# One unit's square, two masks and a turn moved in the delta-rule part of a decoder layer on one core

## The chip, the core and the metric

The kernel runs on one core of a Trainium2 chip. The metric is the device time of one execution in microseconds (us); the time before is the median of 3 runs. The engines are TensorE (PE: matmuls and turns, that is transposes), VectorE (DVE), ScalarE (ACT), GpSimd (POOL) and SyncE (SP, which issues loads). Each takes its instructions in the order of its own list and waits at semaphores for the others.

## The reference, cut to what matters

One inference step of a hybrid decoder layer for 256 prompt tokens and 8 samples of 8 tokens: RMSNorm, one input projection, then two groups of heads side by side (8 attention heads, and 8 heads of a gated delta rule behind a causal convolution of width 4), an output projection, and a convolutional feed-forward part. The change lies in the delta-rule heads:

```
q, k, v = silu(causal_conv4(qkv, conv_w, old_rows))      # and the new old_rows are an output
q = l2norm(q) * 128**-0.5 ; k = l2norm(k)
per chunk of tokens:
  lower = eye + strict(beta * decay * (k @ k.T))
  u  = solve(lower, beta*v - beta*exp(cg) * (k @ s))
  o  = exp(cg) * (q @ s) + (decay * (q @ k.T)) @ u
  s  = exp(g_last) * s + k_dec.T @ u
o = o * rsqrt(mean(o*o) + EPS) * norm_w * silu(z)
```

The solve is done by blocks of 32: the inverse of a lower block is built up over levels 1, 2, 4, 8, 16, and each level needs the entries of the block that a mask of that level lets through. For the samples, with 8 tokens each, levels up to 4 do.

## The kernel before, in words

**Stream.** The weights are streamed in chunks of 512 x 256. SyncE loads a chunk, ACT rounds it to a high part (w_hi, line 821), VectorE subtracts to get the low part (w_lo, line 1173), and TensorE multiplies both parts with a two-part activation: 24 matmuls of 320 columns a chunk (lines 1772 to 1774), each called a product here. The input projection has chunks 0 to 111: g0 (0 to 31) and g1 (32 to 63) feed the delta rule's two groups of four heads, a0 (64 to 87) and a1 (88 to 111) the attention's; then come the output projection (112 to 143) and the feed-forward part.

**Steps between products.** Everything else of the layer is cut into small steps, named by engine and name, as ("P", "kk", g, u): engine P (TensorE), V (VectorE), A (ACT) or G (GpSimd), head group g, unit u. A unit is 128 prompt tokens (u = 0 and 1) or the 64 sample tokens (u = 2, the third unit). `gdn_steps` writes the steps of a group in one order by hand, and `schedule` deals this list out to slots (c, r): chunk c, quarter r. On TensorE a slot's steps stand right behind the six products of that quarter. On the other engines all steps of a chunk follow that chunk's weight conversion (and evacuation of the projection), in the order of the slots; on VectorE the four convolution taps of a pair stand behind the steps of certain quarters.

**The planner's costs.** A chunk counts 40 units. A TensorE step is put into a slot once the units spent have reached the time at which the steps ahead of it are thought ready. A step adds LENGTH x PACE x 1.4 in the delta part, and off TensorE also AHEAD, which is negative for ACT and VectorE (-1) and for GpSimd (-4). "mk" has LENGTH 9, "gs" 7, 10 and 0 on its three engines, "oq" 0. The attention's steps have earliest chunks of their own (group 0 from chunk 82).

**The steps the change touches**, with their lines in the code:
- "kk": TensorE makes k k^T and q k^T of a unit (line 1930 and 1931); VectorE's "kk" (step at line 1375) masks the first by blocks into `a_t_blocks`, makes level 1 in `prod_blocks` and `inv_t_blocks`, and turns blocks (line 1249) into `inv_blocks`; VectorE's "kq" then writes `qk_t`.
- "mk" (GpSimd, line 2332): one level's mask times `a_t_blocks` into `a_t_levels`. TensorE's "pl" of that level (line 1946) reads it; "dx" (line 1956) follows behind a copy by ACT.
- "tk", "tv", "ot" (line 1814 and 2033): turns of k, of v and of the output. "tk" waits for VectorE's "kq", "ot" for VectorE's "o2".
- "sh" (line 2046), "u" (2006), "os" (2021): products with the sample states, the solved values, the output. "us" (2055) with VectorE's "um" and "us": update of the sample states, whose loads and stores GpSimd issues ("si", "s2", "so"). "zm": GpSimd spreads the sample queries (lines 2345 to 2347).
- "o" (ACT, lines 927 and 929): copies the output out of PSUM into `tok_bv`, for u = 0 also squares it into `prod`. For u = 1 and 2 VectorE's "oc" adds the state's part first, and "oq" (ACT, line 934) squares the copy. "o1" (VectorE, 1450) sums the squares, "or" (GpSimd, 2308) takes the root, "o2" scales.
- "gs": TensorE turns the last convolution inputs of all tiles (six turns, line 1814) in the PSUM banks b0 and b1, ACT copies them into `gdn_new_rows` (lines 937 to 939), GpSimd writes them out in seven DMAs (lines 2387 to 2391). It stands ahead of "kk" of group 1's third unit.
- "hk" (GpSimd line 2405): loads the attention's bias table; VectorE's "hk" adds the causal mask to it. "hb" reads it on TensorE, into b2.

The lines that decide the waits spoken of:

```
elif name == "kk":                                    # TensorE
    after(pe, *(("A", "o", g, u - 1) if u else before_group(g)))
    if (g, u) == (1, 2):
        after(pe, "A", "gs")
elif name == "pl":
    after(pe, "G", "mk", *k)
elif name in ("tk", "tv"):
    if name == "tk":
        after(pe, "V", "kq", g, u)
elif name == "gs":
    pe.wait_ge(new_done, 12)
    after(pe, "V", "oc", 1, 1)
```

Of the kernel before, what the change touches and what calls it, by code (L numbers as in the profile page):

```python
# [20 lines left out]
ACT = mybir.ActivationFunctionType  # L21
ALU = mybir.AluOpType
# [163 lines left out]
def gdn_steps(g):  # L186
# [3 lines left out]
    for u in (0, 1, 2):  # L190
        k, nxt = (g, u), (g, u + 1)
        if k == (1, 2):
            s += [("P", "gs"), ("A", "gs"), ("G", "gs")]
        s += [("P", "kk", *k)]
        if u < 2:
            s += [("A", "qs", *nxt)]
        s += [("V", "kk", *k), ("G", "mk", *k, 2)]
        if u == 1:
            s += [("G", "si", g, 0), ("G", "si", g, 1)]
        if u == 2:  # L200
            s += [("G", "mk", *k, 4), ("G", "zm", g), ("G", "si", g, 2)]
        s += [("V", "kq", *k)]
# [31 lines left out]
        if u < 2:  # L234
            s += [("V", "st", *k)]
            if u == 1:
                s += [("G", "so", g, 4)]
        if u:
            s += [("V", "oc", *k), ("A", "oq", *k)]
        if u == 2:  # L240
# [3 lines left out]
    for j in range(4):  # L244
        s += [("P", "us", g, j)] + ([("V", "um", g, j + 1)] if j < 3 else [])
        s += [("V", "us", g, j), ("G", "so", g, j)] + ([("G", "s2", g)] if j == 1 else [])
    return s + tail

# [202 lines left out]
def build(nc, I, O):  # L451
# [213 lines left out]
    def after(e, *key):  # L665

        e.wait_ge(done[key[0]], TALLY[key])
# [69 lines left out]
    with block:  # L737
# [74 lines left out]
        def _(act):  # L812
            def finish(ins):
                ins.then_inc(done["A"], 1)
# [30 lines left out]
            def step(x):  # L845
# [78 lines left out]
                elif name == "o":  # L924
                    rows = out_rows(k[1])
                    after(act, "P", "os", *k)
                    ins = act.activation(bv[rows].rearrange("p h d -> p (h d)"), b2[rows], ACT.Copy)
                    if k[1] == 0:
                        ins = act.activation(pp[rows].rearrange("p h d -> p (h d)"), b2[rows], ACT.Square)
                    finish(ins)  # L930
                elif name == "oq":
                    rows = out_rows(k[1])
                    after(act, "V", "oc", *k)
                    finish(act.activation(pp[rows].rearrange("p h d -> p (h d)"), bv[rows].rearrange("p h d -> p (h d)"), ACT.Square))
# [225 lines left out]
        def _(dve):  # L1160
# [3 lines left out]
            def chain(ins):  # L1164
                link(dve, "V", ins)
# [85 lines left out]
            def step(x):  # L1251
# [123 lines left out]
                elif name == "kk":  # L1375
# [8 lines left out]
                    chain(tt(pc[0:n], atc[0:n], over_heads(C("lev1", n), 4), ALU.mult))  # L1384
                    chain(tt(xtc[0:n], over_heads(C("identB", n), 4), pc[0:n], ALU.subtract))
                    finish(blocks_turn(xc, xtc, n))
                elif name == "kq":
# [58 lines left out]
                elif name == "o1":  # L1446
                    u = k[1]
                    rows = out_rows(u)
                    after(dve, "A", "oq" if u else "o", *k)
                    chain(dve.tensor_reduce(of_sample("so", u, 0, 4), pp[rows, :, :], AX.X, ALU.add))  # L1450
# [309 lines left out]
        def _(pe):  # L1760
# [63 lines left out]
            def step(x):  # L1824
# [96 lines left out]
                elif name == "kk":  # L1921
# [3 lines left out]
                    after(pe, *(("A", "o", g, u - 1) if u else before_group(g)))  # L1925
                    if (g, u) == (1, 2):
                        after(pe, "A", "gs")
                    for h in range(4):
# [4 lines left out]
                elif name == "pl":  # L1933
                    g, u, l = k
                    n = unit(u)[0]
                    after(pe, "G", "mk", *k)
                    if l == 2:
# [120 lines left out]
                elif name == "gs":  # L2058
                    pe.wait_ge(new_done, 12)
                    after(pe, "V", "oc", 1, 1)  # L2060
                    rows = gnew[:, :, :].rearrange("p r f -> p (r f)")
# [40 lines left out]
                elif name == "hb":  # L2102
                    g = k[0]
                    after(pe, "V", "hk", g)
                    after(pe, *(("A", "OT", 0, 1) if g else ("V", "oz", 1, 2)))
                    for h in range(4):
                        ins = pe.matmul(b2[32 * h:32 * h + 32, 0:P + DT], C("rep8"), bm[:, h, 0:P + DT], start=True, stop=True)
# [460 lines left out]
```

## Time and profile before

| | |
|---|---|
| median of 3 runs | 1653.97 us (1653.78 to 1654.66) |
| the profiled execution | 1654.82 us |
| its span, first to last instruction | 1653.1 us |
| mean granted TensorE clock | 0.995 |
| TensorE busy | 1631.2 us (99%), 12899 matmuls |
| VectorE / ACT / GpSimd busy | 64% / 37% / 14% |
| DMA | 256.64 MB, mean 155 GB/s |

A row of a timeline begins with the start in us from the span's first instruction and the duration; "x4" means that four like instructions were merged, and the bracket at its end is how long the engine stood idle before it and what ended that. A matmul's end is modelled, so that neighbours overlap. The table of waits gives total, number and longest wait. PEclk is the granted TensorE clock: 1.00 is 2.4 GHz, 0.50 is 1.2 GHz.

### The profile page before, as it was taken

The page shows a single profiled execution, that of the slowest core. Times are in us where ns is not written, and L with a number is a line of the kernel's source. Part 1 is how long each engine was busy: PE and PEld are TensorE (multiplying, and loading weights), DVE is VectorE, ACT ScalarE, POOL GpSimd, SP SyncE. Part 2 cuts the span into 40 slices and gives each one's busy share as a digit, 9 for nine tenths or more (in the row PEclk, how much of TensorE's full clock was granted, in tenths as well). Part 3 has the DMA queues.
Part 4 walks back from the last instruction along what each step waited for, and adds up shares of the span by engine and source line. Part 5 has one row for each costly group of instructions (what it writes and reads, how often), then busy time and mean ns, then how long its engine had stood idle before and what let it go on. Part 6 is the DMA issues. An engine that isn't in the chain of part 4 may idle for free.

```text
span 1653.1 us, 30926 instructions
## 1 busy us (share of the span) xinstructions
PE 1631.2 (99%) x12899; PEld 1582.5 (96%) x12899; DVE 1050.4 (64%) x1715; ACT 617.2 (37%) x786; POOL 238.0 (14%) x370
## 2 busy tenths in 40 slices
PE   7999999999999999999999999999999999999998
PEld 7999889988998998999999999999999999999997
DVE  5776688656544454776666666666666666666665
ACT  6444333432343343643333333333333333333334
POOL 1122342123212022210000010101010101010004
PEclk9999999999999999999999999999999999999998
DMA  8444354345857467454444444454444444444442
GB/s 246 136 152 124 100 155 140 106 119 146 254 184 251 138 199 238 128 154 150 156 140 155 152 153 148 146 152 153 147 148 153 150 149 148 153 141 156 150 153 84
DMA packets 231243, 256.64 MB, mean 155 GB/s; under 512 B 9444, under 2 KB 220966, under 8 KB 231104
## 3 DMA queue, kind: packets, MB, share of 16 engines
q1 hardware_dynamic: 217856, 220.10, 43.3%
q0 software_dynamic: 10560, 33.29, 6.4%
q8 instruction: 102, 1.67, 0.4%
q10 hardware_dynamic: 2688, 1.27, 0.3%
q14 instruction: 37, 0.30, 0.1%
HBM read 243.50 MB, written 12.69 MB: 155 GB/s over the span
## 4 chain that ended last, share of the span: by engine, by line
PE 93%; DVE 3%; DMA 1%; issue 1%; ACT 0%; POOL 0%; SPq 0%; DVEq 0%; POOLq 0%; ACTq 0%
PE ps_proj L1772 22%; PE ps_proj L1774 22%; PE ps_proj L1773 21%; PE ps_small L1772 6%; PE ps_small L1774 6%; PE ps_small L1773 6%; PE ps_small L1814 2%; DMA k_pages<-in_cache_k_dram 1%; PE ps_small L2046 0%; DMA x_raw<-in_x_sample_dram 0%; PE ps_proj L1814 0%; PE ps_small L1956 0%; PE ps_small L1946 0%; PE ps_small L2152 0%; DMA state_s<-in_state_gdn_dram 0%
## 5 line engine op out<-in xcount | busy, mean ns | idle before, releaser
L1772 PE MATMUL ps_proj<-x_hi,w_hi 128*128 128x320 f32 x2432 | 766.2, 315 | 0.4 <-issue 0.4
L1774 PE MATMUL ps_proj<-x_hi,w_lo 128*128 128x320 f32 x2432 | 752.6, 309 | 0.0
L1773 PE MATMUL ps_proj<-x_lo,w_hi 128*128 128x320 f32 x2432 | 752.3, 309 | 0.0
L821 ACT ACTIVATE w_hi<-w_raw 128x1024 fp32r<-128x1024 f32 x408 | 431.9, 1059 | 740.5 <-PE ps_proj L1774 546.4
L1173 DVE TENSOR_TENSOR w_lo<-w_raw,w_hi 128x1024 fp32r<-128x1024 f32 x408 | 498.1, 1223 | 301.2 <-ACT w_hi L821 300.9
L1772 PEld LDWEIGHTS ps_proj<-x_hi,w_hi 128*128 128x128 f32 x2432 | 457.5, 188 | 14.3 <-issue 10.5
L1773 PEld LDWEIGHTS ps_proj<-x_lo,w_hi 128*128 128x128 f32 x2432 | 457.8, 188 | 0.2
L1774 PEld LDWEIGHTS ps_proj<-x_hi,w_lo 128*128 128x128 f32 x2432 | 457.3, 188 | 0.0
L1772 PE MATMUL ps_small<-hid_hi,w_hi 128*128 128x320 f32 x704 | 218.0, 310 | 0.0
L1774 PE MATMUL ps_small<-hid_hi,w_lo 128*128 128x320 f32 x704 | 217.6, 309 | 0.0
L1773 PE MATMUL ps_small<-hid_lo,w_hi 128*128 128x320 f32 x704 | 217.5, 309 | 0.0
L2512 POOL TENSOR_TENSOR ffn_ext<-ffn_params_t,consts 128x16 f32<-128x16 f32 x88 | 53.6, 630 | 800.3 <-DVE ffn_acc L1632 800.3
L1772 PEld LDWEIGHTS ps_small<-hid_hi,w_hi 128*128 128x128 f32 x704 | 132.1, 188 | 0.2 <-issue 0.2
L1773 PEld LDWEIGHTS ps_small<-hid_lo,w_hi 128*128 128x128 f32 x704 | 132.2, 188 | 0.0
L1774 PEld LDWEIGHTS ps_small<-hid_hi,w_lo 128*128 128x128 f32 x704 | 132.1, 188 | 0.0
L1168 DVE TENSOR_TENSOR x_res<-ps_small,x_res 128x640 f32<-128x640 f32 (+1 forms) x89 | 72.6, 815 | 49.5 <-PE ps_small L1774 49.5
L1632 DVE SCALAR_TENSOR_TENSOR ffn_acc<-ffn_ext,ffn_params_t,ffn_acc 128x336 f32<-128x336 f32 x176 | 94.3, 567 | 3.9
L1168 DVE TENSOR_TENSOR ffn_ext<-ps_proj,root 128x512 f32<-128x512 f32 x132 | 41.7, 372 | 0.0
L1772 PE MATMUL ps_proj<-gated_hi,w_hi 128*128 128x320 f32 x128 | 41.2, 322 | 0.0
L1774 PE MATMUL ps_proj<-gated_hi,w_lo 128*128 128x320 f32 x128 | 39.5, 309 | 0.0
L1773 PE MATMUL ps_proj<-gated_lo,w_hi 128*128 128x320 f32 x128 | 39.5, 309 | 0.0
L1225 DVE SCALAR_TENSOR_TENSOR conv_acc<-u_ext,params_t,conv_acc 128x344 f32<-128x344 f32 x72 | 38.3, 572 | 0.7
(348 smaller groups left out, 1206.7 us busy)
## 6 DMA issues: line engine op xcount, KB each, us to landing
w_raw<-in_w_up_dram SPq DMA_DIRECT2D x176, 512.0 KB, 3.5
w_raw<-in_w_in_dram SPq DMA_DIRECT2D x112, 512.0 KB, 3.9
w_raw<-in_w_down_dram SPq DMA_DIRECT2D x88, 512.0 KB, 3.5
w_raw<-in_w_out_dram SPq DMA_DIRECT2D x32, 512.0 KB, 4.0
k_pages<-in_cache_k_dram POOLq DMA_DIRECT2D x32, 256.0 KB, 3.4
v_pages<-in_cache_v_dram POOLq DMA_DIRECT2D x32, 256.0 KB, 4.3
state_s<-in_state_gdn_dram POOLq DMA_DIRECT2D x10, 512.0 KB, 5.5
out_ss_dram<-state_s POOLq DMA_DIRECT2D x8, 512.0 KB, 4.5
```

Of the source, the lines that this page charges most:

```text
L821: act.activation(whi[:, slot], raw[:, slot], ACT.Copy).then_inc(hi_done, 1)
L1168: return dve.tensor_tensor(out, a_, b_, op)
L1173: dve.tensor_tensor(wlo[:, slot], raw[:, slot], whi[:, slot].bitcast(F32), ALU.subtract).then_inc(lo_done, 1)
L1225: ins = dve.scalar_tensor_tensor(out=acc[:, j, 0:344], in0=u, scalar=wcol, in1=acc[:, j, 0:344], op0=ALU.mult, op1=ALU.add)
L1632: ins = dve.scalar_tensor_tensor(out=facc[:, kind, j, 0:336], in0=u, scalar=w_(tap), in1=facc[:, kind, j, 0:336], op0=ALU.mult, op1=ALU.add)
L1772: pe.matmul(o, hi, rhs_hi[:, k0 + kk_, :], start=first and kk_ == 0, stop=False)
L1773: pe.matmul(o, hi, rhs_lo[:, k0 + kk_, :], start=False, stop=False)
L1774: ins = pe.matmul(o, lo, rhs_hi[:, k0 + kk_, :], start=False, stop=last and kk_ == CQ - 1)
L1814: return pe.transpose(out, in_, C("ident", n, n))
L2512: ins = pool.tensor_tensor(fue[:, kind, j, 2 + SEQ:338].rearrange("p (b s) -> p b s", b=DB)[:, :, 0:2], old, C("ones", P, 16).rearrange("p ...
```

## The change

Three edits in the list of steps, with what belongs to them:
- For unit 0, ACT's "o" ends with the copy, and the Square becomes a step "oq" of its own as for the other units, reading the copy in SBUF and waiting for it. "o1" waits for "oq".
- For the third unit VectorE's "kk" makes the masks of levels 2 and 4 itself, ahead of its block turn; the two "mk" steps of GpSimd go, and "pl" no longer waits for them.
- "gs" leaves its place ahead of "kk" of group 1's third unit and comes at the end of group 1's state updates. It waits for VectorE's third state update, "kk" no longer waits for it, and "hb" of attention group 0 now does.

```
--- before.py
+++ after.py
@@ -189,16 +189,14 @@
     tail = []
     for u in (0, 1, 2):
         k, nxt = (g, u), (g, u + 1)
-        if k == (1, 2):
-            s += [("P", "gs"), ("A", "gs"), ("G", "gs")]
         s += [("P", "kk", *k)]
         if u < 2:
             s += [("A", "qs", *nxt)]
-        s += [("V", "kk", *k), ("G", "mk", *k, 2)]
+        s += [("V", "kk", *k)] + ([("G", "mk", *k, 2)] if u < 2 else [])
         if u == 1:
             s += [("G", "si", g, 0), ("G", "si", g, 1)]
         if u == 2:
-            s += [("G", "mk", *k, 4), ("G", "zm", g), ("G", "si", g, 2)]
+            s += [("G", "zm", g), ("G", "si", g, 2)]
         s += [("V", "kq", *k)]
         if u < 2:
             s += [("P", "nr", *nxt), ("V", "ss", *nxt), ("G", "rn", *nxt)]
@@ -235,8 +233,7 @@
             s += [("V", "st", *k)]
             if u == 1:
                 s += [("G", "so", g, 4)]
-        if u:
-            s += [("V", "oc", *k), ("A", "oq", *k)]
+        s += ([("V", "oc", *k)] if u else []) + [("A", "oq", *k)]
         if u == 2:
             s += [("V", "um", g, 0)]
         s += [("V", "o1", *k), ("G", "or", *k)]
@@ -244,6 +241,8 @@
     for j in range(4):
         s += [("P", "us", g, j)] + ([("V", "um", g, j + 1)] if j < 3 else [])
         s += [("V", "us", g, j), ("G", "so", g, j)] + ([("G", "s2", g)] if j == 1 else [])
+    if g:
+        s += [("P", "gs"), ("A", "gs"), ("G", "gs")]
     return s + tail
 
 
@@ -924,13 +923,10 @@
                 elif name == "o":
                     rows = out_rows(k[1])
                     after(act, "P", "os", *k)
-                    ins = act.activation(bv[rows].rearrange("p h d -> p (h d)"), b2[rows], ACT.Copy)
-                    if k[1] == 0:
-                        ins = act.activation(pp[rows].rearrange("p h d -> p (h d)"), b2[rows], ACT.Square)
-                    finish(ins)
+                    finish(act.activation(bv[rows].rearrange("p h d -> p (h d)"), b2[rows], ACT.Copy))
                 elif name == "oq":
                     rows = out_rows(k[1])
-                    after(act, "V", "oc", *k)
+                    after(act, *(("V", "oc", *k) if k[1] else ("A", "o", *k)))
                     finish(act.activation(pp[rows].rearrange("p h d -> p (h d)"), bv[rows].rearrange("p h d -> p (h d)"), ACT.Square))
                 elif name == "gs":
                     after(act, "P", "gs")
@@ -1383,6 +1379,9 @@
                     chain(ins)
                     chain(tt(pc[0:n], atc[0:n], over_heads(C("lev1", n), 4), ALU.mult))
                     chain(tt(xtc[0:n], over_heads(C("identB", n), 4), pc[0:n], ALU.subtract))
+                    if u == 2:
+                        for i in range(2):
+                            tt(lev[0:n, i], atc[0:n], over_heads(C(f"lev{LEVELS[i + 1]}", n), 4), ALU.mult)
                     finish(blocks_turn(xc, xtc, n))
                 elif name == "kq":
                     g, u = k
@@ -1446,7 +1445,7 @@
                 elif name == "o1":
                     u = k[1]
                     rows = out_rows(u)
-                    after(dve, "A", "oq" if u else "o", *k)
+                    after(dve, "A", "oq", *k)
                     chain(dve.tensor_reduce(of_sample("so", u, 0, 4), pp[rows, :, :], AX.X, ALU.add))
                     finish(dve.scalar_tensor_tensor(out=of_sample("ro", u, 0, 4), in0=of_sample("so", u, 0, 4), scalar=1.0 / P,
                                                     in1=of_sample("eq", u, 4 * u, 4 * u + 4), op0=ALU.mult, op1=ALU.add))
@@ -1923,8 +1922,6 @@
                     n, c0 = unit(u)
                     pe.wait_ge(silu_done, 6 * g + 4)
                     after(pe, *(("A", "o", g, u - 1) if u else before_group(g)))
-                    if (g, u) == (1, 2):
-                        after(pe, "A", "gs")
                     for h in range(4):
                         kT_ = reg[g][:, 4 + h, c0:c0 + n]
                         pe.matmul(b1[0:n, h * n:(h + 1) * n], kT_, kT_, start=True, stop=True)
@@ -1933,7 +1930,8 @@
                 elif name == "pl":
                     g, u, l = k
                     n = unit(u)[0]
-                    after(pe, "G", "mk", *k)
+                    if u < 2:
+                        after(pe, "G", "mk", *k)
                     if l == 2:
                         after(pe, "V", "kk", g, u)
                         if u:
@@ -2057,7 +2055,7 @@
                     finish(ins)
                 elif name == "gs":
                     pe.wait_ge(new_done, 12)
-                    after(pe, "V", "oc", 1, 1)
+                    after(pe, "V", "us", 1, 2)
                     rows = gnew[:, :, :].rearrange("p r f -> p (r f)")
                     for r in range(6):
                         n = min(P, 648 - r * P)
@@ -2103,6 +2101,8 @@
                     g = k[0]
                     after(pe, "V", "hk", g)
                     after(pe, *(("A", "OT", 0, 1) if g else ("V", "oz", 1, 2)))
+                    if g == 0:
+                        after(pe, "A", "gs")
                     for h in range(4):
                         ins = pe.matmul(b2[32 * h:32 * h + 32, 0:P + DT], C("rep8"), bm[:, h, 0:P + DT], start=True, stop=True)
                     finish(ins)
```

## Rows read from the trace of the kernel before

**Rows 1.** Page, parts 1 and 4: engine shares, and the chain that ended last.
```profile
PE 1631.2 (99%) x12899; PEld 1582.5 (96%) x12899; DVE 1050.4 (64%) x1715; ACT 617.2 (37%) x786; POOL 238.0 (14%) x370
...
PE 93%; DVE 3%; DMA 1%; issue 1%; ACT 0%; POOL 0%; SPq 0%; DVEq 0%; POOLq 0%; ACTq 0%
```
**Rows 2.** Waits of TensorE: total us, times, longest.
```profile
PE ps_small L1946 <- POOL a_t_levels L2332: 1.3, 1, 1.3
PE ps_small L1814 <- DVE tok_bv L1431: 0.9, 1, 0.9
...
PE ps_small L1930 <- ACT prod L929: 0.8, 2, 0.4
PE ps_small L1930 <- ACT gdn_new_rows L939: 0.7, 1, 0.7
```
**Rows 3.** Timeline of ACT, first group, end of unit 0.
```profile
152.22 0.60 ACT L927 ACTIVATE tok_bv<-ps_small 128x512 f32<-128x512 f32 x1 [2.14 <-PE ps_small L2025]
152.71 0.59 ACT L929 ACTIVATE prod<-ps_small 128x512 f32<-128x512 f32 x1
```
**Rows 4.** Timeline of VectorE, first group, masks of the third unit.
```profile
201.63 1.22 DVE L1173 TENSOR_TENSOR w_lo<-w_raw,w_hi 128x1024 fp32r<-128x1024 f32 x1
202.76 0.57 DVE L1168 TENSOR_TENSOR a_t_blocks<-ps_small,decay 32x128 f32<-32x128 f32 x2
203.37 0.28 DVE L1168 TENSOR_TENSOR prod_blocks<-a_t_blocks,consts 64x128 f32<-64x128 f32 x1
...
204.34 0.42 DVE L1168 TENSOR_TENSOR qk_t<-ps_small,decay 64x256 f32<-64x256 f32 x1
```
**Rows 5.** Timeline of TensorE, first group, same stretch.
```profile
203.00 0.31 PE L1774 MATMUL ps_proj<-x_hi,w_lo 128*128 128x320 f32 x1
203.15 0.31 PE L1772 MATMUL ps_proj<-x_hi,w_hi 128*128 128x320 f32 x1
...
204.91 0.60 PE L1814 MATMUL ps_small<-consts,reg 128*64 128x128 f32 x4
206.86 0.44 PE L1946 MATMUL ps_small<-inv_blocks,a_t_levels 32*32 32x32 f32 x16 [1.35 <-POOL a_t_levels L2332]
```
**Rows 6.** Timeline of TensorE, second group, around "gs" and "kk".
```profile
368.35 0.31 PE L1774 MATMUL ps_proj<-x_hi,w_lo 128*128 128x320 f32 x1
...
371.94 0.30 PE L1930 MATMUL ps_small<-reg 128*64 128x64 f32 x2 [0.68 <-ACT gdn_new_rows L939]
...
372.99 0.41 PE L1772 MATMUL ps_proj<-x_hi,w_hi 128*128 128x320 f32 x1
```
**Rows 7.** Timeline of VectorE, second group, the split ahead of "kk".
```profile
370.89 1.22 DVE L1173 TENSOR_TENSOR w_lo<-w_raw,w_hi 128x1024 fp32r<-128x1024 f32 x1
```
**Rows 8.** Timeline of GpSimd: row stores of "gs"; bias load "hk".
```profile
374.12 2.69 POOL L2391 DMA_DIRECT2D out_gcs_dram<-gdn_new_rows  x5
...
422.16 0.77 POOL L2405 DMA_DIRECT2D bias_q<-rb_copies  x1
```
**Rows 9.** Timeline of VectorE at the bias load.
```profile
428.78 0.69 DVE L1168 TENSOR_TENSOR bias_q<-bias_q,consts 128x512 f32<-128x512 f32 x1 [4.29 <-DMA bias_q<-rb_copies]
429.39 2.35 DVE L1173 TENSOR_TENSOR w_lo<-w_raw,w_hi 128x1024 fp32r<-128x1024 f32 x2
```
**Rows 10.** Timeline of TensorE, first product of chunk 85.
```profile
435.46 0.31 PE L1772 MATMUL ps_proj<-x_hi,w_hi 128*128 128x320 f32 x1
```
**Rows 11.** Stretches: length, busy us by engine, granted clock, DMA share, GB/s.
```profile
94.80:97.10 2.30, 2.30 (x21) 2.22 (x20) 0.36 (x3) 1.05 (x1) 0.00 (x0) 1.00 0.00 0
261.30:263.90 2.60, 2.54 (x20) 2.46 (x21) 1.10 (x6) 1.29 (x2) 0.00 (x0) 1.00 1.00 302
264.40:267.90 3.50, 3.50 (x17) 3.50 (x16) 2.77 (x4) 2.35 (x4) 0.91 (x1) 0.51 0.05 17
275.00:277.80 2.80, 2.80 (x55) 2.59 (x54) 2.19 (x9) 0.01 (x1) 0.01 (x1) 1.00 0.39 106
278.10:281.50 3.40, 3.40 (x44) 3.00 (x42) 2.58 (x4) 3.12 (x5) 3.26 (x5) 0.50 0.09 33
```

More of the change, by code:

```diff
@@ L191, in gdn_steps @@
         k, nxt = (g, u), (g, u + 1)
-        if k == (1, 2):
-            s += [("P", "gs"), ("A", "gs"), ("G", "gs")]
         s += [("P", "kk", *k)]
@@ L196, in gdn_steps @@
             s += [("A", "qs", *nxt)]
-        s += [("V", "kk", *k), ("G", "mk", *k, 2)]
+        s += [("V", "kk", *k)] + ([("G", "mk", *k, 2)] if u < 2 else [])
         if u == 1:
@@ L200, in gdn_steps @@
         if u == 2:
-            s += [("G", "mk", *k, 4), ("G", "zm", g), ("G", "si", g, 2)]
+            s += [("G", "zm", g), ("G", "si", g, 2)]
         s += [("V", "kq", *k)]
@@ L237, in gdn_steps @@
                 s += [("G", "so", g, 4)]
-        if u:
-            s += [("V", "oc", *k), ("A", "oq", *k)]
+        s += ([("V", "oc", *k)] if u else []) + [("A", "oq", *k)]
         if u == 2:
@@ L246, in gdn_steps @@
         s += [("V", "us", g, j), ("G", "so", g, j)] + ([("G", "s2", g)] if j == 1 else [])
+    if g:
+        s += [("P", "gs"), ("A", "gs"), ("G", "gs")]
     return s + tail
@@ L926, in step @@
                     after(act, "P", "os", *k)
[L927 to L930, printed above, removed]
+                    finish(act.activation(bv[rows].rearrange("p h d -> p (h d)"), b2[rows], ACT.Copy))
                 elif name == "oq":
                     rows = out_rows(k[1])
-                    after(act, "V", "oc", *k)
+                    after(act, *(("V", "oc", *k) if k[1] else ("A", "o", *k)))
                     finish(act.activation(pp[rows].rearrange("p h d -> p (h d)"), bv[rows].rearrange("p h d -> p (h d)"), ACT.Square))
@@ L1385, in step @@
                     chain(tt(xtc[0:n], over_heads(C("identB", n), 4), pc[0:n], ALU.subtract))
+                    if u == 2:
+                        for i in range(2):
+                            tt(lev[0:n, i], atc[0:n], over_heads(C(f"lev{LEVELS[i + 1]}", n), 4), ALU.mult)
                     finish(blocks_turn(xc, xtc, n))
@@ L1448, in step @@
                     rows = out_rows(u)
-                    after(dve, "A", "oq" if u else "o", *k)
+                    after(dve, "A", "oq", *k)
                     chain(dve.tensor_reduce(of_sample("so", u, 0, 4), pp[rows, :, :], AX.X, ALU.add))
@@ L1925, in step @@
                     after(pe, *(("A", "o", g, u - 1) if u else before_group(g)))
-                    if (g, u) == (1, 2):
-                        after(pe, "A", "gs")
                     for h in range(4):
@@ L1935, in step @@
                     n = unit(u)[0]
-                    after(pe, "G", "mk", *k)
+                    if u < 2:
+                        after(pe, "G", "mk", *k)
                     if l == 2:
@@ L2059, in step @@
                     pe.wait_ge(new_done, 12)
-                    after(pe, "V", "oc", 1, 1)
+                    after(pe, "V", "us", 1, 2)
                     rows = gnew[:, :, :].rearrange("p r f -> p (r f)")
@@ L2105, in step @@
                     after(pe, *(("A", "OT", 0, 1) if g else ("V", "oz", 1, 2)))
+                    if g == 0:
+                        after(pe, "A", "gs")
                     for h in range(4):
```

## The prediction

> **What bounds the kernel now.** I read the page's shares first: TensorE is busy for 99% of the span and makes up 93% of the chain that ended last [rows 1]. So the time is what TensorE has to do, plus what it waits, plus what a lower clock costs it. The change removes nothing from TensorE and adds nothing to it, as the six turns of "gs" only move. It can act in two ways: through TensorE's waits, and through its granted clock.
>
> Next the table of waits. Behind the first load, TensorE waits some 5 us in all, and the edit is aimed at four entries: 0.8 us in two waits of "kk" for the Square of ACT line 929, 1.3 for the level masks of GpSimd, 0.9 for the VectorE rows in front of "gs", and 0.7 for the copies of "gs" [rows 2]. Together that is 0.8 + 1.3 + 0.9 + 0.7 = 3.7 us. If they all went and nothing came, 3.7 us (0.22%) would be the whole gain. A measurement of this kernel can tell about 0.2%, 3.3 us, from no change.
>
> **First unit's square from its copy.** Before, "o" was copy and Square, and "kk" of the next unit waited 0.4 us for the Square's end, 152.71 + 0.59 = 153.30. The copy ends at 152.22 + 0.60 = 152.82 [rows 3], 0.48 earlier, so both waits go: minus 0.8 us. The Square becomes a step of its own behind the copy, on the same queue. Before, it began 0.11 ahead of the copy's end; now it waits for that end, so it comes 0.1 to 0.2 us later, and "o1" on VectorE with it. The next TensorE step that needs VectorE's work on the second unit stands in (32,2), six quarters behind "kk" in (31,0), 5.3 us of products alone; I put the delay at nothing, and at 0.2 without that cover.
>
> **Level masks on VectorE.** Two masks of 64x128 come into "kk" ahead of its transpose. The same shape took 0.28 us there [rows 4], so 0.56 us a group, in front of "kq", "o2" and the following weight split on VectorE's queue. GpSimd loses two masks a group and does "zm" and the state load "si" earlier; they only gain room.
>
> What decides is where the planner then puts the next TensorE steps. A mask counted 9 x 1.4 - 4 = 8.6 units there, and a quarter of a chunk, six products, is 10. Two masks fewer are 17.2 units, and worked out for the changed list they have this effect: in the first group "tk" and "pl" of the third unit go from slot (40,2) to (40,0), two quarters or 12 products earlier. TensorE takes a product each 0.147 us (203.00 to 203.15, and 0.88 a quarter), so it stands at "tk" not at 204.91 but 1.76 us earlier, at 203.15 [rows 5]. "tk" waits for VectorE's "kq". VectorE's order is held by its queue: weight split at 201.63, "kk" from 202.76, "kq" from 204.34 to 204.76, and 0.56 later with the masks: 205.32 [rows 4]. None of this hangs on GpSimd or on the new place. So TensorE waits from 203.15 to 205.32, 2.2 us, where it had waited 1.35 one step later [rows 5]; the profile counts idleness from the modelled end of the last matmul, 0.31 - 0.15 = 0.16 later, so 2.0 in its rows. **The wait for GpSimd becomes a longer wait for VectorE**: plus 0.65 us. Behind it "pl" and "ot" find masks and "o2" done.
>
> **Turn of the old rows at the group's end.** Without "gs" ahead of it, "kk" of the third unit starts near 368.35 + 0.15 = 368.5, takes 1.05 (371.94 to 372.99), and "tk", now in (72,0) instead of (72,3) ("gs" had counted 17.3 units more), comes 18 products later: 368.5 + 1.05 + 2.65 = 372.2 [rows 6]. VectorE has its weight split at 370.89, held by "o1" and not by TensorE [rows 7]; adding what followed that split in the first group (201.63 to 204.76, 3.13) and the masks' 0.56 gives "kq" done at 374.6 [rows 4, 7]. Wait: 2.4 us, 2.2 in the profile's counting, against 0.9 + 0.7 = 1.6 removed: plus 0.6.
>
> At its new place, (80,1), the turn needs VectorE's third state update, whose product stands nine quarters, 7.9 us, ahead of it in (78,0), so it costs its own work and no wait. "ot" of the third unit comes a quarter behind and finds "o2" just done; I take nothing, bounds 0 to 0.5. On ACT the three copies leave the stretch at 371 and stand near 418, with nothing waiting close behind. On GpSimd seven DMA issues move: five took 2.69 us, so seven about 3.8. They leave the place ahead of "zm" and of the state loads and stores, which gain that room, and now stand between the last state store and the bias load "hk" [rows 8]. VectorE waits for that load in order (4.29 us at 428.78), with two weight splits behind it [rows 9]. The first of them ends at 429.39 + 1.18 = 430.6, and TensorE needs it for chunk 85, at 435.46 [rows 10]: 4.9 us of cover. Counted from the last state product, I estimate that the load is issued 5.3 us later (3.8 of issues, and 1.5 until the turn and its copies are done) and that chunk 85 comes 3.4 us later (the state products stand three quarters earlier, 2.6, and the turn's 0.8 lies between): 4.9 - 5.3 + 3.4 = 3.0 us of cover stay. Nothing is charged. SP's weight loads keep their places; the moved 0.3 MB of rows shares the DMA engines with them.
>
> **Sum of the waits**: removed 3.7, new 2.0 + 2.2 = 4.2: plus 0.5 us, bounds minus 0.6 and plus 1.3 (below, the masks' 0.56 hidden in both groups; above, "ot" and the last "os" of the first group waiting a few tenths: there "ks" comes ahead of a convolution tap on VectorE, whose SiLU stands before the copy of "u" on ACT).
>
> **The clock.** TensorE ran at half its level, 1.2 instead of 2.4 GHz, in two stretches, 264.4 to 267.9 and 278.1 to 281.5; each cost half its length, 1.7 us [rows 11]. Ahead of each lay the one-column norm matmuls. The same matmuls at 94.8 brought no fall, and neither did the 1.35 us wait [rows 5, 11], so it doesn't come with a step alone. The two new waits, 2.2 and 2.4 us with a few small products behind, leave TensorE with less to do than any of these. From two falls in four such stretches I put the chance of a fall behind each new wait at a little over one half. Old falls may go as well as come, since all behind 152 shifts by tenths.
>
> The Trainium skill, TensorE: Matmul & The Clock Gate, Part 1, says that TensorE goes back to half clock after a stretch without work, judged on a clock that runs by itself and doesn't restart with the kernel. By that rule no new fall would come, and the sum would stay at plus 0.5. The trace disagrees on the first point: both falls came behind stretches that were busy for 2.54 of 2.60 and 2.80 of 2.80 us.
>
> **The cases.** The profiled execution took 1654.82 us, of which 1653.1 is the span; the median of the runs shown is 1653.97, 0.85 lower. I add to the median.
> - Forecast: waits as summed, and one fall more: 0.5 + 1.7 = plus 2.2, 1656.2 us (1657.0 against the profiled execution). Chance 0.35.
> - As many falls as now: plus 0.5, 1654.5 us. For it: the 1.35 us wait brought none. It is also what the skill's rule gives. Chance 0.29.
> - **Slower**: the level falls behind both new waits: 0.5 + 3.4 = plus 3.9, 1657.9 us. It decides once both waits reach 2 us and fall badly in time; against it, two of four earlier stretches were spared. Chance 0.17.
> - One fall fewer, because the norm matmuls shift: 0.5 - 1.7, 1652.8 us. Chance 0.09.
> - **Faster**: VectorE has "kq" ready at the earlier place, and only the removals count: minus 3.7, 1650.3 us. Against it stands VectorE's queue, where the split lies ahead of "kk" in both groups [rows 4, 7]. Chance 0.05.
> - The bias load comes more than 3.0 us later than I count, behind the seven DMAs, and TensorE stands at chunk 85 for the rest, 1 to 3 us on top: about 1658.5. Chance 0.05.
> - That the edit doesn't do what it says: TensorE still waits at "kk", as the copy alone is too late. That leaves 0.8 us more, inside the other cases.
>
> The first three hold 0.81, so the range is theirs with the bounds of the terms: 1653.6 to 1658.4. Faster by over 0.2% is only the case of the waits gone, with a little for what I missed: 0.06. Slower by over 0.2% (above 1657.3) is the two falls and the late load: 0.22. The rest, 0.72, is no change that can be told.
>
> **What the changed kernel's profile would show.** Right: no wait of "kk" for ACT; no wait of "pl" for GpSimd; in both groups a wait of about 2 us of the "tk" turns for VectorE's qk_t product; "gs" near 418 without a wait; VectorE's wait for the bias load up to 2 us longer on TensorE's count, with no TensorE wait at chunk 85; three stretches at half level. Wrong: "tk" waits of under 1 us (the faster case), a TensorE wait on w_lo behind 430 (the late load), or another number of half-level stretches (the clock cases).

## The result and the profile after

The changed kernel took 1655.17 us (median of 20 runs), the kernel before 1652.41 beside it (20 runs): a ratio of 1.0015, 95% interval 1.0009 to 1.0021, that is 2.5 us more (1.5 to 3.5). In a later comparison it was 1655.38 to 1653.36, 1.0010 (1.0001 to 1.0019). The forecast was plus 2.2 us. The size fits and the cause does not: the waits rose by more than was counted (plus 2.3 us for plus 0.5), and the added half-level stretch didn't come. The time itself came out 1 us under the forecast 1656.2, as that was counted from a median of three runs, 1653.97.

| | before | after |
|---|---|---|
| profiled execution | 1654.82 us | 1655.73 us |
| its span | 1653.1 us | 1654.0 us |
| TensorE busy | 1631.2 us | 1629.6 us |
| span less busy | 21.9 us | 24.4 us |
| half-level stretches before the last chunks | 2 | 1 |

The page of the changed kernel, parts 1 and 4, answers to [rows 1]:

```profile
PE 1629.6 (99%) x12899; PEld 1581.5 (96%) x12899; DVE 1050.0 (63%) x1719; ACT 617.8 (37%) x786; POOL 237.3 (14%) x366
...
PE 93%; DVE 4%; DMA 1%; issue 1%; POOL 0%; ACT 0%; DVEq 0%; SPq 0%; POOLq 0%
```

With the same 12899 matmuls TensorE is busy for 1.6 us less: there is one half-level stretch fewer, and the last turns ran at full level, where they ran at half level before (under "The clock"). It is idle for 2.5 us more. The two together, 0.9, are the whole difference of the two profiled executions. The table of TensorE's waits, as in [rows 2], names the idle time:

```profile
PE ps_small L1813 <- DMA x_raw<-in_x_sample_dram: 7.7, 2, 6.4
PE ps_small L1813 <- DVE qk_t L1164: 3.8, 2, 1.9
PE ps_small L2031 <- DVE tok_bv L1164: 2.5, 2, 1.6
PE ps_small L1813 <- DMA k_pages<-in_cache_k_dram: 0.6, 1, 0.6
```

All four entries that the edit aimed at are gone, 3.7 us. In their place stand "tk", waiting for `qk_t`, 3.8 us, and "ot" of the third unit, waiting for "o2" (`tok_bv`), 2.5 us. In the same list of the kernel before that "ot" had 0.3 us:

```profile
PE ps_small L2033 <- DVE tok_bv L1168: 0.3, 1, 0.3
```

So the waits come to minus 3.7, plus 3.8, plus 2.2: plus 2.3 us.

**The "tk" waits** came as forecast. TensorE, first group, the answer to [rows 5]:

```profile
203.16 0.31 PE L1773 MATMUL ps_proj<-x_hi,w_lo 128*128 128x320 f32 x1
205.36 1.02 PE L1813 MATMUL ps_small<-consts,reg 128*64 128x128 f32 x4 [1.89 <-DVE qk_t L1164]
206.31 0.64 PE L1944 MATMUL ps_small<-inv_blocks,a_t_levels 32*32 32x32 f32 x16
```

VectorE in the same stretch, the answer to [rows 4]:

```profile
201.77 1.22 DVE L1169 TENSOR_TENSOR w_lo<-w_raw,w_hi 128x1024 fp32r<-128x1024 f32 x1
202.91 0.57 DVE L1164 TENSOR_TENSOR a_t_blocks<-ps_small,decay 32x128 f32<-32x128 f32 x2
...
204.15 0.48 DVE L1164 TENSOR_TENSOR a_t_levels<-a_t_blocks,consts 64x128 f32<-64x128 f32 x2
...
204.88 0.42 DVE L1164 TENSOR_TENSOR qk_t<-ps_small,decay 64x256 f32<-64x256 f32 x1
```

The split is where it was (201.77, before 201.63), the two masks take 0.48 us, and "kq" ends at 205.30 in place of 204.76. TensorE's last product ahead of "tk" starts at 203.16, where before there were twelve more. In the second group "tk" starts at 373.71 behind the same 1.90 us of idleness. "pl" follows "tk" at once: VectorE has only taken GpSimd's place in the line of waits.

**The "ot" wait of the second group** is the longest new one that the sum had no term for. TensorE, and VectorE in the same stretch:

```profile
419.31 0.31 PE L1773 MATMUL ps_proj<-x_hi,w_lo 128*128 128x320 f32 x1
421.27 0.46 PE L2031 MATMUL ps_small<-consts,tok_bv 64*128 64x64 f32 x4 [1.65 <-DVE tok_bv L1164]
```

```profile
416.15 1.23 DVE L1164 TENSOR_TENSOR state_s<-state_s,small 128x1024 f32<-128x1024 f32 x1 [3.17 <-DMA state_s<-in_state_gdn_dram]
417.41 1.22 DVE L1164 TENSOR_TENSOR state_s<-ps_small,state_s 128x1024 f32<-128x1024 f32 x1
418.55 1.22 DVE L1169 TENSOR_TENSOR w_lo<-w_raw,w_hi 128x1024 fp32r<-128x1024 f32 x1
419.68 0.82 DVE L1164 TENSOR_TENSOR reg<-ps_proj,consts 128x640 f32<-128x640 f32 x1
420.53 0.69 DVE L1164 TENSOR_TENSOR tok_bv<-tok_bv,small 64x512 f32<-64x512 f32 x1
```

Read it from the bottom. "o2" (420.53) ends at 421.22, and "ot" starts. Ahead of it lie an evacuation and a split, since the planner put "o2" into chunk 80 (it follows the moved turn in the list). Ahead of those lies the last state update, which stood 3.17 us for the load "s2" of its state. TensorE's steps come three quarters sooner, which moves this update from chunk 80 to chunk 79, ahead of one split and one evacuation more: VectorE reaches it at 412.98 and not at 418.51. The load didn't come as much sooner. GpSimd's row in the changed kernel, and the landing times of this line's ten loads before and after:

```profile
407.66 0.89 POOL L2370 DMA_DIRECT2D state_s<-in_state_gdn_dram  x1
```

```profile
L2370 POOL DMA_DIRECT2D state_s<-in_state_gdn_dram x10: 884/901/995, 158.2 to 411.1; - x10
...
DMA to landing us min/median/max: 4.6/5.5/7.2
```

```profile
L2370 POOL DMA_DIRECT2D state_s<-in_state_gdn_dram x10: 882/897/979, 158.7 to 407.7; - x10
...
who waited for it (us, times):
  DVE state_s L1164: 3.2, 1
...
DMA to landing us min/median/max: 4.7/5.4/8.4
```

It was issued 3.5 us sooner (the last load, 411.1 to 407.7) and took 8.4 us in place of 7.2, each time the longest of the ten. So it landed 2.3 us sooner for an update that came 5.5 us sooner. In the first group "ot" waits 0.83 us, at 252.09: it went from (48,3) to (48,1), and VectorE's "o2" stayed in chunk 47. There the load had landed, and VectorE was still at its splits and updates.

**The clock.** The stretches of [rows 11] in the changed kernel, with the one behind the first "tk" wait:

```profile
205.40:208.90 3.50, 3.50 (x29) 2.98 (x30) 3.50 (x7) 0.27 (x1) 3.32 (x6) 0.51 0.37 102
264.40:267.90 3.50, 3.50 (x28) 3.42 (x28) 1.87 (x7) 0.64 (x1) 1.03 (x1) 1.00 0.30 102
278.10:281.50 3.40, 3.40 (x82) 3.00 (x81) 3.30 (x11) 2.72 (x4) 1.98 (x3) 1.00 0.52 154
```

The granted clock (third number from the right) is at half level behind the first "tk" wait, and full behind the norm matmuls, where it had fallen before.

What a fall costs is read from the same steps with and without it. From "tk" to the first "sh" they took 6.21 us in the changed kernel and 4.71 us in e5_ot_later, which had no fall there: 1.5 us.

```profile
205.36 1.02 PE L1813 MATMUL ps_small<-consts,reg 128*64 128x128 f32 x4 [1.89 <-DVE qk_t L1164]
211.57 1.08 PE L2044 MATMUL ps_small<-state_s,reg 128*32 128x128 f32 x32
```

```profile
205.07 0.63 PE L1814 MATMUL ps_small<-consts,reg 128*64 128x128 f32 x4 [1.89 <-DVE qk_t L1165]
209.78 1.08 PE L2045 MATMUL ps_small<-state_s,reg 128*32 128x128 f32 x32
```

Read in the same way against e8_before_again, which had none, the two falls of the kernel before cost 1.6 and 1.25 us. The clock also falls at the very end of every profile. There TensorE has next to nothing left to do: the kernel before ran its last eight turns at half level, and the changed kernel at full.

```profile
1643.57 1.97 PE L2251 MATMUL ps_proj<-consts,x_normed 128*64 128x128 f32 x8
```

```profile
1644.47 1.09 PE L2251 MATMUL ps_proj<-consts,x_normed 128*64 128x128 f32 x8
```

That is 0.9 us here (1.2 in e6_both_later, where the clock fell sooner). But in the mean granted clock this end stretch weighs 2.2 to 5.0 us in the 13 profiles (half its length inside the span), more than a fall, so the mean does not count falls.

**The rest.** The turn stands at 417.93 with no wait, and the bias load is issued behind its seven DMAs, at 423.74 (before 422.16, [rows 8]). VectorE waits 4.52 us for it, ending at 429.74 (4.29 and 428.78 in [rows 9]). TensorE doesn't wait for it: behind 425 us its list has only 0.6 us for an attention load and 0.4 of issue.

### The profile page after: what moved, and what is told of

It reads as the page before. It is cut to its first block, busy times and chain, and to the rows that moved or that the text cites. A ratio compares the mean times of both kernels' runs of the same rounds, so it can differ in the third digit from the quotient of the medians.

```text
span 1654.0 us, 30924 instructions
## 1 busy us (share of the span) xinstructions
PE 1629.6 (99%) x12899; PEld 1581.5 (96%) x12899; DVE 1050.0 (63%) x1719; ACT 617.8 (37%) x786; POOL 237.3 (14%) x366
## 4 chain that ended last, share of the span: by engine, by line
PE 93%; DVE 4%; DMA 1%; issue 1%; POOL 0%; ACT 0%; DVEq 0%; SPq 0%; POOLq 0%
PE ps_proj L1771 22%; PE ps_proj L1773 21%; PE ps_proj L1772 21%; PE ps_small L1771 6%; PE ps_small L1772 6%; PE ps_small L1773 6%; PE ps_small L1813 2%; DVE w_lo L1169 1%; DVE state_s L1164 1%; DMA state_s<-in_state_gdn_dram 1%; PE ps_small L2044 0%; PE ps_small L2134 0%; PE ps_small L2152 0%; PE ps_small L1944 0%; PE ps_small L1954 0%
```

## The experiments

Two causes were to be told apart: the waits of "tk" and "ot", microsecond for microsecond, and the clock's falls. Since the falls differ from run to run, the table also has an estimate at equal clock: within one kernel the time falls by about 1.0 us for each 0.001 of the mean granted clock (pooled over the 222 runs of the comparisons; single kernels give between nothing and 1.7), so each run's time is put to a mean clock of 0.997 by that price, and averaged. It is an estimate, as the mean holds the end stretch too. "Idle" is span less busy of the profiled run, against 21.9 before. The estimates of before are 1653.1 (35 runs), 1653.3 (30) and 1653.6 (21); the differences in the table have standard errors of 0.25 to 0.55.

| experiment | median (runs) | ratio, 95% | idle | estimate at equal clock, against before |
|---|---|---|---|---|
| e1_square | 1653.09 (12) | 0.9999 (0.9990 to 1.0007) | +0.2 | +0.1 |
| e2_masks | 1654.20 (11) | 1.0006 (0.9998 to 1.0015) | +1.4 | +1.7 |
| e3_turn | 1654.32 (12) | 1.0005 (0.9996 to 1.0014) | +0.3 | +0.4 |
| e8_before_again | 1653.58 (11) | 1.0006 (0.9997 to 1.0015) | 0.0 | +0.5 |
| e4_tk_later | 1649.59 (9) | 0.9978 (0.9968 to 0.9988) | -1.6 | -3.0 |
| e5_ot_later | 1654.27 (11) | 1.0002 (0.9992 to 1.0011) | -0.5 | -0.5 |
| e6_both_later | 1650.53 (11) | 0.9983 (0.9974 to 0.9992) | -2.8 | -3.0 |
| e7_load_sooner | 1653.80 (11) | 1.0001 (0.9992 to 1.0010) | +1.1 | -0.1 |
| e9_after_again | 1655.38 (11) | 1.0010 (1.0001 to 1.0019) | +4.2 | +2.6 |
| e10_ot_sooner | 1659.42 (6) | 1.0038 (1.0025 to 1.0051) | +4.6 | +5.0 |
| e11_ot_later_again | 1653.24 (11) | 1.0001 (0.9991 to 1.0010) | +0.1 | -0.5 |

The first four were compared with 1653.04 us of the kernel before, the next four with 1653.35, the last three with 1653.36. A few waits early in the kernel differ between runs of one program (in the list of e9_after_again the first load's two waits take 9.0 us for 7.7, and one of 0.8 is new), which is why its idle time is 1.7 above that of the first profile of the same kernel.

### One part alone

**e1_square**: the first edit alone, on the kernel before.

```
-        if u:
-            s += [("V", "oc", *k), ("A", "oq", *k)]
+        s += ([("V", "oc", *k)] if u else []) + [("A", "oq", *k)]
```

> The first edit alone (the Square of unit 0 from its copy). No slot moves. Theory of the waits: the two waits of kk for ACT, 0.4 us each, go, and nothing comes: minus 0.8 us, ratio 0.9995. Rival (the clock makes the difference): no change beyond the noise, 1.000, and no wait of the list has to change with the time.

The two waits of "kk" for the Square left the list of waits. In the time the 0.8 us isn't to be seen (0.9999): the runs differ by more. The changed kernel shows why the copy is enough; ACT, first group, answering to [rows 3], and TensorE's "kk":

```profile
152.83 0.60 ACT L926 ACTIVATE tok_bv<-ps_small 128x512 f32<-128x512 f32 x1 [2.14 <-PE ps_small L2023]
153.46 0.63 ACT L930 ACTIVATE prod<-tok_bv 128x512 f32<-128x512 f32 x1
```

```profile
153.36 0.31 PE L1773 MATMUL ps_proj<-x_hi,w_lo 128*128 128x320 f32 x1
153.57 0.46 PE L1927 MATMUL ps_small<-reg 128*128 128x128 f32 x2
```

The copy ends at 153.43, "kk" starts at 153.57.

**e2_masks**: the second edit alone.

```
-        s += [("V", "kk", *k), ("G", "mk", *k, 2)]
+        s += [("V", "kk", *k)] + ([("G", "mk", *k, 2)] if u < 2 else [])
```

> The second edit alone (masks of the third unit on VectorE). The steps from tk on stand two quarters earlier. Theory of the waits: GpSimd's 1.35 us go; tk waits 1.9 us for VectorE's qk_t in the first group and nothing in the second, where the turn of the old rows still delays kk; ot waits 0.8 us in the first group and 0 to 1.5 in the second. Together plus 1.1 to plus 2.6 us, ratio 1.0007 to 1.0016. Rival (the move itself is free, the clock pays): minus 1.35 us from the removed wait, 0.999, plus 1.7 us only in runs with one more stretch at half level.

```profile
PE ps_small L1817 <- DVE qk_t L1168: 1.9, 1, 1.9
PE ps_small L2037 <- DVE tok_bv L1168: 1.4, 2, 0.8
```

The wait for GpSimd's masks (1.3) is gone, a "tk" wait of 1.9 us stands in the first group alone, and "ot" waits 1.4. In the second group the turn still stands ahead of "kk", and "tk" (374.96) waits for nothing. By these rows the edit costs minus 1.3, plus 1.9, plus 1.1, or 1.7 us; the ratio gives 1.0, its interval holding no change, and the estimate at equal clock 1.7.

**e3_turn**: the third edit alone.

```
-        if k == (1, 2):
-            s += [("P", "gs"), ("A", "gs"), ("G", "gs")]
...
+    if g:
+        s += [("P", "gs"), ("A", "gs"), ("G", "gs")]
```

> The third edit alone (turn of the old rows at the end of the second group). In the second group the steps from tk on stand one quarter earlier. Theory of the waits: 0.9 + 0.7 us go; in the second group ot now comes behind the turn and waits about 1.6 us for VectorE's o2, and pl 0 to 1.5 us for the masks of GpSimd: 0 to plus 1.5 us, ratio 1.0000 to 1.0009. Rival (the turn's move only removes waits): minus 1.6 us, 0.9990.

```profile
PE ps_small L1944 <- POOL a_t_levels L2332: 2.7, 2, 1.3
...
PE ps_small L2031 <- DVE tok_bv L1168: 0.2, 1, 0.2
```

The turn's 1.6 us went, and the second group's "pl" now waits for GpSimd's masks as the first one's did: 1.3 us more. The "ot" wait that was expected of this edit alone didn't come: here "ot" stands in (81,0), and in (80,2) in the changed kernel, two quarters sooner, while "o2" belongs to chunk 80 in both and VectorE takes it behind that chunk's split. So the long "ot" wait of the second group needs the second edit too, which draws TensorE's steps forward.

**e8_before_again**: the kernel before, unchanged, to see what a comparison makes of no change.

> The kernel before, unchanged, as a run of its own: 1.000 within 0.001 by every theory. It shows how the granted clock and the time of the same program spread. The clock rival needs a mean granted clock here above that of the changed kernel (0.9976 over its 20 runs) by about 0.001, which is one half-level stretch; the theory of the waits needs the same mean within 0.0005.

It gave 1.0006, so a single ratio is good to about 0.001, 1.6 us, and none of the three edits can be told from no change by its ratio alone. By their rows they do add up: minus 0.8, plus 1.7, minus 0.3 are 0.6, and the rest of the 2.3 is what the second and third edit do together in the second group (there "tk" 1.9 and "ot" 1.65 stand in place of the 1.3 and 0.2 of e3_turn and the 0.5 of "ot" in e2_masks).

### The waits taken away

All four are the changed kernel with one edit more; no instruction is added or left out.

**e4_tk_later**: the planner counts 26 units more for VectorE's "kk" of the third unit, which does more now.

```
+        more = {('V', 'kk', 0, 2): 26, ('V', 'kk', 1, 2): 26}.get((x[0], x[1]) + x[2:4], 0)
-        return LENGTH[x[0]].get(x[1], 5) * PACE[x[0]] * SPREAD["attention" if x in attention else "delta"]
+        return LENGTH[x[0]].get(x[1], 5) * PACE[x[0]] * SPREAD["attention" if x in attention else "delta"] + more
```

> The changed kernel, but the planner counts 26 units more for VectorE's kk of the third unit, so that tk and all behind it stand three quarters later (40,3) and (72,3). Theory of the waits: the two waits of tk, 1.9 us each, go to under 0.2; ot's waits stay in sum between 1.0 and 2.5 us, as its distance to the last state update is the same. Minus 3 to minus 5 us against the changed kernel, ratio to before 0.998 to 0.9995. Rival (VectorE's work as a whole is what TensorE waits for): the time saved at tk comes back at ot and nothing is won, 1.0015.

"tk" goes three quarters later, to (40,3) and (72,3), and starts at 207.16 and 372.92 without a wait. What stays is one "ot" wait, in the first group, and "pl" behind "tk" there now waits 0.3 us for VectorE's block turn:

```profile
PE ps_small L2032 <- DVE tok_bv L1165: 1.5, 1, 1.5
```

The ratio is 0.9978: 3.6 us below the kernel before, and 0.37% or 6 us below the changed kernel by the two ratios, for 3.8 + 1.0 us of waits removed. That is more than the 3 to 5 us expected, and more than the rows account for, though the two intervals leave room for that; at equal clock it is 5.6.

**e5_ot_later**: 20 units more for "o2" of the third unit in the same way; "ot" goes two quarters later.

```
+        more = {('V', 'o2', 0, 2): 20, ('V', 'o2', 1, 2): 20}.get((x[0], x[1]) + x[2:4], 0)
```

> The changed kernel, but the planner counts 20 units more for VectorE's o2 of the third unit, so that only ot stands two quarters later, (48,3) and (81,0). Theory of the waits: ot's 0.8 and 1.65 us go to under 0.3 in sum, tk's 3.8 stay: minus 2.2 to minus 2.5 us against the changed kernel, ratio to before 1.0000. Rival (one more stretch at half level is what was added): no gain from a later ot, 1.0015.

No wait of "ot" is left, the "tk" waits are as they were:

```profile
PE ps_small L1814 <- DVE qk_t L1165: 3.8, 2, 1.9
```

**e6_both_later**: both.

```
+        more = {('V', 'kk', 0, 2): 26, ('V', 'kk', 1, 2): 26, ('V', 'o2', 0, 2): 20, ('V', 'o2', 1, 2): 20}.get((x[0], x[1]) + x[2:4], 0)
```

> The changed kernel with both planner costs. Theory of the waits: neither tk nor ot waits, all that the edit removed stays removed: minus 3.5 to minus 4 us against the kernel before, ratio 0.9976 to 0.998, the fastest of all. Rival (VectorE as a whole is late): as before, 1.000, with the waits at another step. Rival (clock): the gain is under 2 us.

Neither wait is left. Against e5_ot_later, measured with it, the "tk" wait of 3.8 us is gone (small waits of 0.3 and 0.5 us came), and the medians differ by 1654.27 - 1650.53 = 3.7 us, or 2.6 at equal clock. Against e4_tk_later it should have been faster by 1.5 us; it was 0.9 slower, and at equal clock the same. So the last "ot" wait's price doesn't show in this pair.

**e7_load_sooner**: the load "s2" ahead of the state store of the same step on GpSimd's queue; "ot" keeps its place.

```
-        s += [("V", "us", g, j), ("G", "so", g, j)] + ([("G", "s2", g)] if j == 1 else [])
+        s += [("V", "us", g, j)] + ([("G", "s2", g)] if j == 1 else []) + [("G", "so", g, j)]
```

> The changed kernel, but GpSimd issues the last state load (s2) ahead of the second state store instead of behind it. Theory of the waits, with the load as the cause of ot's wait in the second group: the load is issued some 2 us sooner, VectorE's wait of 3.2 us for it shrinks to about 1, ot's wait there from 1.65 to 0.2 or less; the first group's 0.8 stays, where the load had landed: minus 1.4 us against the changed kernel, ratio to before 1.0006. Rival (VectorE's own queue, weight split and evacuation ahead of o2, is the cause): ot's wait stays above 1 us, 1.0015.

VectorE in the second group, and TensorE's list of waits:

```profile
414.85 1.23 DVE L1164 TENSOR_TENSOR state_s<-state_s,small 128x1024 f32<-128x1024 f32 x1 [1.44 <-PE ps_small L2053]
...
419.24 0.69 DVE L1164 TENSOR_TENSOR tok_bv<-tok_bv,small 64x512 f32<-64x512 f32 x1
```

```profile
PE ps_small L1813 <- DVE qk_t L1164: 3.8, 2, 1.9
...
PE ps_small L2031 <- DVE tok_bv L1164: 0.8, 1, 0.8
```

The update no longer waits for the load (its 1.44 us is for TensorE), and the second group's "ot" wait of 1.65 is gone with nothing else moved; the first group's 0.8 stays. That shows the load as that wait's cause. The time, 1.0001, lies on that side too.

### The third unit's output turn, in three places

What "ot" costs was the smaller effect, so the changed kernel ran again beside two that differ from it in the place of "ot" alone: minus 20 units for "o2", and plus 20.

```
+        more = {('V', 'o2', 0, 2): -20, ('V', 'o2', 1, 2): -20}.get((x[0], x[1]) + x[2:4], 0)
```

**e9_after_again**, **e10_ot_sooner** and **e11_ot_later_again**:

> The changed kernel once more, beside two that differ from it in the place of the third unit's ot alone. Waits theory: ot waits about 2.5 us in its two places, tk 3.8; ratio to the kernel before 1.0014 (+2.3 us). Rival (the average is set by the clock's falls and the ot waits cost nothing): ratio the same as that of the two others.

> The changed kernel with ot of the third unit put two quarters sooner in the first group and one in the second. VectorE's o2 keeps its place. Waits theory: three quarters of products, 3 x 0.88 = 2.6 us, become waits: ot waits about 5.1 us, the time is 2.6 us above that of the changed kernel, ratio to before about 1.003. Rival: the same time as the changed kernel.

> The changed kernel with ot of the third unit put two quarters later in each group. Waits theory: no ot wait, 2.2 us below the changed kernel of the same call, ratio to before about 1.000. Rival: the same time as the changed kernel.

The "ot" waits in the three lists are 2.2, 4.8 (the row below) and none; "tk" has 3.8 in each.

```profile
PE ps_small L2032 <- DVE tok_bv L1165: 4.8, 2, 2.6
```

From 0 to 2.2 to 4.8 us of waits the medians go 1653.24, 1655.38, 1659.42: steps of 2.1 and 4.0 us, at equal clock 3.2 and 2.4, for waits of 2.2 and 2.6. The steps are uneven by a microsecond or more, as the runs are, but the direction holds in both counts. Over the whole way it is 6.2 or 5.6 us for 4.8. The rival, that these waits cost nothing, falls.

The falls didn't follow the waits in this way. e9_after_again had two, 1.6 and 0.5 us behind the ends of its two "tk" waits (busy and granted clock of the stretch of the first wait, and behind it):

```profile
205.40:208.20 2.80, 1.31 (x24) 1.08 (x24) 2.73 (x7) 0.27 (x1) 2.74 (x4) 1.00 0.62 187
208.20:212.00 3.80, 3.80 (x31) 3.40 (x30) 3.57 (x10) 0.00 (x1) 2.05 (x6) 0.55 0.61 177
```

Counted over all 13 profiles, and leaving out the stretch at the kernel's very end: 13 "tk" waits of 1.9 us brought 5 falls, one fall stood behind the 2.6 us "ot" wait of e10_ot_sooner, and 6 behind the norm matmuls. Those seven profiles that had "tk" waits show 8 falls, the six without show 4, too few to tell whether the waits add falls on average. The mean granted clock over the runs is no lower with them: 0.9976 and 0.9978 for the changed kernel (20 and 11 runs), 0.9971, 0.9969 and 0.9972 for the kernel before (35, 30, 21). But it holds the end stretch, which weighs 2.3 and 2.2 us in the changed kernel's two profiles and 4.8 and 2.6 in those of the kernel before, and that alone could make the difference.

## Why the prediction was right, and where it was wrong

- **The bound, and the four waits removed**: right. TensorE stayed at 99%, and the 3.7 us went.
- **Square from the copy**: right. The Square follows the copy by 0.03 us, where I had 0.1 to 0.2, and nothing waits for it.
- **Masks on VectorE, and "tk" two quarters earlier**: right, with its mechanism. "tk" was to wait 2.0 us in the profile's counting and waited 1.89; the masks took 0.48 for my 0.56. Behind it "pl" and the second unit's "ot" waited for nothing, as said. e4_tk_later and e6_both_later showed that this wait, and not VectorE's added work, is the cost: the work is still there and the time is won back.
- **"tk" in the second group**: right, 1.90 for my 2.2.
- **The moved turn, and the bias load**: right; no wait at either.
- **The step that failed** is "'ot' of the third unit comes a quarter behind and finds 'o2' just done; I take nothing, bounds 0 to 0.5". For the third unit's "ot" of the first group, which comes two quarters sooner too, the sum had no term at all. "ot" waits 2.5 us, 1.65 and 0.83, where it had waited 0.3. I followed the places of TensorE's steps and took it that VectorE's come along. In the first group "o2" keeps its chunk. In the second the update ahead of "o2" does come forward, and stands: it needs a 512 KB load, whose issue moved by 3.5 us and whose landing by 2.3, while the update's own place moved by 5.5; then "o2" stood behind another chunk's split and evacuation. The waits' sum was plus 2.3, outside my bounds of minus 0.6 to plus 1.3.
- **The clock term failed too.** "One fall more", plus 1.7, isn't in the time. The waits give plus 2.3 by the rows; the two comparisons gave 2.5 (1.5 to 3.5) and 1.7 (0.2 to 3.1), and the estimate at equal clock 2.6. That leaves about nothing for the clock, and the profiled run had one fall fewer. A fall behind a new wait is real, 5 in 13 where I had said a little over one half. But my sum let the old falls stand, and they aren't fixed to a place: the unchanged kernel had two in one profile (264 and 278) and none in another (e8_before_again). The chance was also taken from too few stretches: the norm matmuls stand in six places (in the kernel before at 94.8, 106.8, 160.7, 261.4, 275.0 and 330.2 us), of which I had counted three. And a fall cost 1.25 to 1.6 us where it was read, not 1.7. Whether the changed kernel has more or fewer falls on average stays open.
- The two errors, plus 1.8 for the waits and about minus 1.7 for the clock, nearly cancel, so that the predicted size fits is luck. The range is also a little narrower than the bounds named for it give (1653.4 to 1658.7), which changes nothing here.
- The rivals: the case of the same number of falls, plus 0.5, had the clock nearer the truth, with waits too low by 1.8. The late bias load and the waits simply gone are ruled out by the profile. Falls behind both new waits came in one of the two profiles of the changed kernel (e9_after_again), so they are possible, but they are not the usual case.

## What to carry to other kernels

When work moves from one engine to another, the cost that a planner counts for it must move along: here the same instructions, with 26 units put down for VectorE, turned plus 2.5 us into minus 3.6. A step that is drawn forward brings its wait with it unless everything that its producer needs, loads included, comes forward as far; so follow each moved step back to the last DMA on the producer's queue before costing it at nothing. A drop in clock that comes and goes between runs of one program is a spread around the result, to be averaged over many runs of both kernels, and no term to be added from one profile; and the mean granted clock counts low stretches that cost next to nothing, like the one at the kernel's end.

## What the runs showed that was not expected

- In a kernel whose TensorE is busy for 99% of the time, the runs of one program spread by 5 us (1650.72 to 1656.05 for the kernel before), and the granted clock goes with it: in the changed kernel's 20 runs the time falls by 1.2 us for each 0.001 of clock. Half-level stretches stood behind the norm matmuls at 111, 264, 276 or 278 us, behind a wait of 1.9 or 2.6 us, or nowhere, in different profiles. The Trainium skill, TensorE: Matmul & The Clock Gate, Part 1, says that the clock is judged in a rhythm that runs by itself and doesn't restart with the kernel, so that the same kernel counts more or fewer slow matmuls from run to run. These profiles agree that it differs between runs; the rhythm itself no run here shows. The Trainium skill there ties the lower level to a time without work, and half of the falls here (6 of 12) followed norm matmuls in which TensorE was busy throughout, as in [rows 11].
- Eight of the ten 512 KB state loads took 4.6 to 6.1 us to land (the kernel before, the changed kernel in both its profiles, e3_turn and e7_load_sooner). The last of each group is issued right behind a state store of the same size and took 6.4 to 6.7 us in the first group and 7.0 to 8.4 in the second. Issued ahead of that store (e7_load_sooner, at 406.29 for 407.66 in the second group), it took 4.9 and 5.1.
